# Value projections of an attention stage, set 256 columns wide for a pair of heads

## The reference, cut to what matters

```python
def diff_attention(h, w_in, lam_q1, ..., w_out, layer_idx):
    qkv = h @ w_in                                  # 256 x 1024 @ 1024 x 3072
    q, k, v = jnp.split(qkv, 3, axis=-1)
    q = q.reshape(B, S, H, 2, dh) * (dh ** -0.5)    # 8 heads, two halves of 64
    k = k.reshape(B, S, H, 2, dh)
    v = v.reshape(B, S, H, dv)                      # dv = 128
    ...
        a = softmax(s1) - lam * softmax(s2)         # per block of 128 queries
        return einsum('bhqk,bkhd->bqhd', a, v)
    ...
    o = rmsnorm(o, subln_g) * (1.0 - lam_init)
    return o.reshape(B, S, H * dv) @ w_out
```

## Time and profile before

| what | value |
|---|---|
| median of three runs | 1293.92 us |
| the profiled execution's own time | 1294.76 us |
| its span, first to last instruction | 1292.6 us |
| PE busy | 1035.1 us (80%) |
| DVE busy | 463.6 us (36%) |
| ACT busy | 235.9 us (18%) |
| mean granted TensorE clock | 0.905 |
| HBM traffic over the span | 314 GB/s |

### The profile page before, as it was taken

One profiled execution on the slowest core, in us unless ns is written; L12 is line 12 of the kernel. 1 busy time (PEld: TensorE's weight loads), 2 busy tenths in 40 slices (PEclk: granted clock), 3 DMA queues, 4 the chain that ended last, 5 costly groups with the idle time before them and its releaser, 6 DMA issues.

```text
span 1292.6 us, 15349 instructions
## 1 busy us (share of the span) xinstructions
PE 1035.1 (80%) x6075; PEld 605.6 (47%) x6075; DVE 463.6 (36%) x1142; ACT 235.9 (18%) x575; POOL 43.0 (3%) x91
## 2 busy tenths in 40 slices
PE   4899997999999979989999999694654647474647
PEld 1788844444333456856788685451212113131213
DVE  1369824232222246876853463521010101010211
ACT  2133312111111131224521200120101010010101
POOL 0000000000000020000010500000000000000000
PEclk9899897999999979989999999898878778786878
DMA  9785935999999969711314108789999999999997
GB/s 370 246 335 196 396 112 213 371 429 427 427 427 428 429 236 388 292 66 66 131 38 139 67 23 308 298 329 425 423 424 423 422 427 419 429 421 428 421 428 292
DMA packets 76892, 406.10 MB, mean 314 GB/s; under 512 B 18633, under 2 KB 19974, under 8 KB 54184
## 3 DMA queue, kind: packets, MB, share of 16 engines
q1 hardware_dynamic: 76840, 405.38, 77.5%
HBM read 403.14 MB, written 2.23 MB: 314 GB/s over the span
## 4 chain that ended last, share of the span: by engine, by line
PE 30%; DMA 25%; DVE 6%; issue 1%; ACT 0%; SPq 0%; POOL 0%; DVEq 0%
DMA ring<-in_expert_w_up 11%; DMA ring<-in_expert_w_gate 7%; DMA ring<-in_expert_w_down 7%; PE ps L1247 5%; PE ps L2663 3%; PE ps L1884 3%; PE ps L3139 2%; PE ps L1287 2%; PE ps L2911 1%; PE ps L3129 1%; PE ps L1263 1%; PE ps L2032 1%; PE ps L1228 1%; PE ps L2742 1%; PE ps L2675 1%
## 5 line engine op out<-in xcount | busy, mean ns | idle before, releaser
L1247 PE MATMUL ps<-ring,hT_sb 128*32 128x512 f32 x672 | 127.8, 743 | 163.1 <-DMA side<-in_expert_w_gate 53.6
L1247 PEld LDWEIGHTS ps<-ring,hT_sb 128*32 128x32 f32 x672 | 32.8, 133 | 252.5 <-issue 252.5
L1620 PE MATMUL ps<-ring,hT_sb 128*64 128x512 f32 x448 | 113.2, 595 | 3.4 <-DMA ring<-in_expert_w_gate 3.4
L1374 DVE TENSOR_TENSOR tmp<-ps,tmp 128x512 f32<-128x512 f32 x8 | 5.5, 692 | 194.7 <-ACT tmp L1362 194.7
L644 PE MATMUL ps<-hT_sb,ring 128*128 128x256 f32 x256 | 62.3, 393 | 4.1 <-DMA ring<-in_attn_w_in 4.1
L1247 PE MATMUL ps<-side,hT_sb 128*32 128x512 f32 x224 | 61.3, 710 | 0.0
L1620 PEld LDWEIGHTS ps<-ring,hT_sb 128*64 128x64 f32 x448 | 35.4, 137 | 55.0 <-issue 54.9
L1353 ACT ACTIVATE hT_sb<-ps,modc 128x128 f32<-128x128 f32 x72 | 27.1, 457 | 181.4 <-PE ps L1228 181.4
L1884 PE MATMUL ps<-hT_sb,ring 128*128 128x256 f32 (+1 forms) x240 | 59.8, 405 | 0.0
L1628 PE MATMUL ps<-ring,tmp 128*64 128x512 f32 x256 | 56.7, 595 | 0.0
L644 PEld LDWEIGHTS ps<-hT_sb,ring 128*128 128x128 f32 x256 | 48.0, 194 | 15.3 <-issue 4.6
(11 more groups left out here) (510 smaller groups left out, 1628.5 us busy)
## 6 DMA issues: line engine op xcount, KB each, us to landing
ring<-in_expert_w_down SPq DMA_DIRECT2D x24, 2048.0 KB, 16.5
ring<-in_expert_w_gate SPq DMA_DIRECT2D x12, 4096.0 KB, 20.7
ring<-in_expert_w_up SPq DMA_DIRECT2D x12, 4096.0 KB, 31.7
ring<-in_expert_w_up SPq DMA_DIRECT2D x16, 2048.0 KB, 18.5
ring<-in_expert_w_down SPq DMA_DIRECT2D x7, 4096.0 KB, 19.9
ring<-in_expert_w_gate SPq DMA_DIRECT2D x12, 2048.0 KB, 19.6
side<-in_ada_w SPq DMA_DIRECT2D x20, 1024.0 KB, 6.3
ring<-in_w_in SPq DMA_DIRECT2D x9, 2048.0 KB, 8.0
```

The source lines that it names most:

```text
L1247: last = pe.matmul(bank[es, :], xg[:, c, es], w[e][:, c, :], start=(c == 0), stop=(c == KC - 1))
L1620: last = pe.matmul(bank[e * SLOTS:(e + 1) * SLOTS, :], xg[:, c, e * SLOTS:(e + 1) * SLOTS], dst(e, j, par)[:, c, :], start=(c == 0), stop= ...
```

## The change

`project_v` now takes one token block for two heads at a time: j = h // 2 is the pair, t = h % 2 the token block. A matmul is 256 columns wide (the weight columns of two neighbouring heads) and there are 8 of them an iteration where there were 16. The even iteration computes token block 0 of heads h and h+1, the odd one token block 1 of heads h-1 and h. The 8 matmuls are cut into two halves of 4 by channel chunks. PSUM bank 7 is used in full: the even iteration writes its first 256 columns, the odd one the last 256, and ACT copies the half of that iteration.

In an even iteration the halves stand where the two token blocks stood. In an odd iteration the first half moves up, between the halves of K's projection, and the second half stands where token block 0 stood; nothing is left between `av(a)` and `av(b)`. `av` waits for `v_out` of the odd iteration of its head's pair.

```diff
-                def project_v(h, t):
-
-                    if t == 0:
+                def project_v(h, half):
+
+                    j, t = h // 2, h % 2
+                    if t == 0 and half == 0:
                         if h % 4 == 0:
                             pe.wait_ge(sem(f"m1_loaded{4 + h // 4}"), 16)
-                        if h:
-                            pe.wait_ge(sem("v_out"), h)
-                    for c in range(KC):
-                        last = pe.matmul(ps[7][:, t * P:(t + 1) * P], hT[:, c, t * P:(t + 1) * P],
-                                         cell(4 + h // 4)[:, c, (h % 4) * P:(h % 4 + 1) * P],
+                    if half == 0 and h:
+                        pe.wait_ge(sem("v_out"), h)
+                    for c in range(4 * half, 4 * half + 4):
+                        last = pe.matmul(ps[7][:, t * S:(t + 1) * S], hT[:, c, t * P:(t + 1) * P],
+                                         cell(4 + j // 2)[:, c, j % 2 * S:(j % 2 + 1) * S],
                                          start=(c == 0), stop=(c == KC - 1))
-                    if t:
+                    if half:
                         last.then_inc(sem("v_psum"), 1)
...
-                    pe.wait_ge(sem("v_out"), h + 1)
+                    pe.wait_ge(sem("v_out"), 2 * (h // 2) + 2)
...
                     project_qk(h, 1, 0)
+                    if h % 2:
+                        project_v(h, 0)
                     project_qk(h, 1, 1)
                     if h:
                         turn(a)
-                    project_v(h, 0)
+                    project_v(h, h % 2)
                     if h:
                         turn(b)
                         if h == 1:
                             pe.wait_ge(sem("colsB_done"), 1)
                         av(a)
-                    project_v(h, 1)
+                    if h % 2 == 0:
+                        project_v(h, 1)
                     if h:
                         av(b)
...
-                        act.activation(v3[:, :, h * P:(h + 1) * P], ps[7][:, 0:S].rearrange("p (t d) -> p t d", t=NT),
+                        act.activation(v3[:, h % 2, h // 2 * S:(h // 2 + 1) * S], ps[7][:, h % 2 * S:(h % 2 + 1) * S],
                                        ACT.Copy).then_inc(sem("v_out"), 1)
```

## The result

| | before | changed |
|---|---|---|
| median, 17 runs each | 1294.4 us | 1302.98 us |
| lowest to highest | 1291.57 to 1298.96 | 1298.75 to 1304.82 |
| profiled execution, time (span) | 1294.76 (1292.6) | 1299.01 (1296.9) |

The ratio of the changed kernel to the one before is 1.0058, with a 95% interval from 1.0046 to 1.0071: 0.6% slower, 7.5 us (6.0 to 9.2). The medians alone lie 8.6 us apart: the changed kernel's executions gather near 1299 and near 1304 us, and its median falls into the second group. The forecast was 1301 us and +6.6.

The account below looks back on a forecast made before the run. PE was taken to bound the attention loop. Odd iterations +6.6 us, even ones -0.5 and DVE's lateness +0.5 gave +6.6 us on 1294.76, so 1301 us; range 1296 to 1307.

Parts of the forecast that it names:

- The bound: Attention loop: PE is busy all 13.47 us of an iteration, so a pause of PE lengthens it one for one.
- The wide matmuls: V projection: 3.45 us instead of 3.58 for a head's share, saving 0.13 us an iteration, 1.0 us in all.
- The first pause: Odd iterations, before `av(a)`: PE waits for ACT's copy of V, 1.20 us from `turn(b)`; pause 1.0 us.
- The second pause: Odd iterations, before `av(b)`: PE waits for DVE to empty bank 5, 1.15 us after `av(a)`; pause 0.7 us.
- My low bound for the whole: Smallest total change by the bounds of the terms: 4 x 1.3 - 0.5 = +4.8 us.
- Odd iterations: Iterations h = 1, 3, 5, 7: each +1.65 us, to near 15.1 us; four of them +6.6 us.
- DVE late at h = 6: First `turn` of iteration 6: held by DVE, 0.75 us late, costing 0.5 us (0 to 0.7).
- Pass-through: From attention to the end: the delay goes through at full size, first refill of the experts' cells at about 231.8.
- The rival in which the delay is absorbed: Downstream of attention: a transfer is what is waited for, the 6.6 us vanish, 1295 us; chance 0.12.
- The clock: Rival, odd iterations: pauses halve PE's clock in one to three of four, 1.7 us each, 1303 to 1307; chance 0.15.
- The loads as the pace: Rival, V projection: weight loads set the pace, so halving them saves 14.3 us, net -6.7 us, 1288; chance 0.04.

Follow-up runs that it names:

- copy_first: Changed kernel with ACT copying V ahead of `take_turned(b)` in odd iterations; ratio 1.0046 to the kernel before.
- earlier: Changed kernel with each pair's V projected one iteration earlier, so the wide matmuls need no wait; ratio 1.0019 to the kernel before.
- narrow: Changed kernel's order and waits, but V projected by 16 matmuls of 128 columns an iteration; ratio 1.0050 to the kernel before.
- again: The changed kernel run a second time, no edit; ratio 1.0062 to the kernel before.
- both_waits: Changed kernel with ACT copying V ahead of `take_turned(b)` and `av(b)` of odd iterations in bank 7; ratio 1.0026 to the kernel before.

## Why the prediction was right, point by point

The test of the mechanism is the loop, +6.50 us and the same in two traces. That the median also came within 2 us of 1301 is partly luck, since executions of the changed kernel lie between 1298.75 and 1304.82 us.

- *The bound.* PE has no slack in the loop: every pause lengthened its iteration one for one, and `copy_first` gave back 0.49 us for each of 4 copies moved. That the stage's end is DVE's, and not PE's, I had not seen: the earlier trace rows show it in their bracket, and I used them only as a bound of the second pause. It did not touch the forecast, for in the changed kernel DVE is held up along with PE; it did undo the gain of `earlier`.
- *The wide matmuls.* 0.13 us an iteration was forecast. Even iterations went from 13.47 to 13.35, and `narrow` cost 0.84 us over seven. Sixteen records take 1.73 + 1.73 = 3.46 us where 3.45 was reckoned. Right in kind and size.
- *The first pause.* 1.20 us forecast from `turn(b)` to `av(a)`, 1.17 to 1.22 measured.
- *The second pause.* 1.15 us from `av(a)` to `av(b)`, 1.16 measured. Of the two ends the lower was the right one: DVE had been idle for 2.22 us in h = 1. My low bound for the whole, written as 4 x 1.3 - 0.5 = +4.8, adds up to 4.7; nothing hangs on it.
- *Odd iterations.* 15.1 us forecast, 15.10 to 15.14 measured.
- *DVE late at h = 6.* 0.5 us forecast; the iteration is 0.32 us longer than the other even ones. DVE began its part of h = 6 at 123.71 us, 3.22 us into the iteration where 2.58 was due: 0.64 late and not 0.75. The load's lead on its matmul took up 0.2 of that, as allowed. The slack was more than the 0.1 allowed: DVE's last step had ended 0.23 us ahead of the load, and the hand-over took 0.05 here (129.26 to 129.31), so 0.18. The first transpose came 0.26 us late, and the second's load, exposed behind it, cost 0.06 more. It is the term furthest from its forecast.
- *Pass-through.* In `again`, whose iteration 0 is like that of the trace before, the refill came at 231.82 us, 6.65 later than in the earlier trace rows, and the span is 6.7 longer. From the last `av` to the end there are 1134.4 and 1134.7 us in the two traces of the changed kernel, 1134.7 before. The rival in which the delay is absorbed is gone: the mechanism of the first refill, released by PE, carried it whole.
- *The clock.* No fall inside the loop in two traces (1.00 in all iterations from h = 1 on). The rival priced this at one to three falls; it did not happen there, and the measured 7.5 us does not need it, since 6.5 lies in its interval of 6.0 to 9.2. By the median of 1302.98 us alone it could not be told from the forecast, since its range began at 1303; the traces decide it.
- *The loads as the pace.* Gone with `narrow`.

What stays open: by the ratio the time moved 1 us more than the loop did, by the medians 2.1. The interval covers the first, but of the changed kernel only executions of 1299.01 and 1301.41 us were traced. Its nine longest executions (1302.98 us and more) have a mean granted clock of 0.895 to 0.899, the seven below 1300 us one of 0.899 to 0.904; where in the execution the long ones lose it is not shown.

## What to carry to other kernels

Before widening an operation, read the pace of the narrow one from its starts: records of 128 columns 112 ns apart and of 256 columns 216 ns apart say that the columns are the cost, and then nothing is left to win but 0.13 us a head. What the edit moves is worth more than what it widens: work that stood between a producer and its consumer was the cover of a wait, here 1.79 us of matmuls over a copy of 0.28. If a pair of heads is to share an operation, finish the pair one iteration before its first use, and see which engine ends the stage before counting the gain.

## What the runs showed that I had not expected

The tail behind the attention stage can take longer though no edit aims at it. `both_waits` was traced in a long execution (1301.87 us, where its median is 1295.84): its tail from the last `av` is 1138.9 us, that of the kernel before 1134.7 and of `again` 1134.7. Most of the difference arises between 381 and 509 us behind the last `av`, in the second block's mixers. That part of `both_waits` and then of `again` (stages, columns as in the earlier trace rows):

```profile
542.00:670.00 128.00, 117.56 (x587) 90.80 (x587) 95.06 (x246) 47.52 (x111) 7.74 (x15) 0.92 0.22 77
```

```profile
546.00:673.00 127.00, 114.85 (x620) 89.83 (x618) 99.85 (x265) 48.59 (x116) 7.75 (x15) 0.97 0.23 80
```

The mean granted clock there is 0.92 against 0.97, and fewer instructions fit into the stretch (587 records of PE against 620). The mean clock over this whole execution is 0.896, like that of the changed kernel's long ones; that they lose their time in the same place is a guess. So an execution can lose some 4 us far from the edit, as much as most of the edits are worth: single times of this kernel tell little below 5 us, while the same stretch of two traces of the changed kernel agreed to 0.01 us.
